# One step's shift of the compressed exponential's followers in the samples' attention of a hybrid decoder kernel

## The reference

```
s_c = einsum(q, k_cmp) * scale                       # compressed scores, 63 blocks
p_c = masked_softmax(s_c)                            # the compressed exponential
o_c = einsum(p_c, v_cmp)
imp = einsum(p_c, overlap)                           # importance of each block of 64 rows
score = where(forced, 1e9, where(future, -1e9, imp))
_, idx = top_k(score, 8)                             # which blocks are attended
s_s = einsum(q, gathered k_sel)                      # here: all scores, with a mask from the top 8
p_s = masked_softmax(s_s)                            # the selected exponential
o_s = einsum(p_s, gathered v_sel)
p_w, o_w = the same over the last 256 rows           # window branch
o = gate_c * o_c + gate_s * o_s + gate_w * o_w
```

## Time and profile before

| what | value |
|---|---|
| median of 3 runs | 4016.66 us (4012.67 to 4022.57) |
| profiled execution, its own time | 4024.7 us |
| its span | 4022.5 us |
| PE busy / PEld busy | 3844.9 us (96%) / 3509.6 us (87%) |
| DVE busy / ACT busy / POOL busy | 50% / 28% / 42% |
| mean granted TensorE clock | 0.978 of full |

### The profile page before, as it was taken

One profiled execution on the slowest core, in us unless ns is written; L12 is line 12 of the kernel. 1 busy time (PEld: TensorE's weight loads), 2 busy tenths in 40 slices (PEclk: granted clock), 3 DMA queues, 4 the chain that ended last, 5 costly groups with the idle time before them and its releaser, 6 DMA issues. The chain is left out here.

```text
span 4022.5 us, 83836 instructions
## 1 busy us (share of the span) xinstructions
PE 3844.9 (96%) x34280; PEld 3509.6 (87%) x34280; DVE 2019.4 (50%) x4755; ACT 1114.4 (28%) x2470; POOL 1695.1 (42%) x2284
## 2 busy tenths in 40 slices
PE   8998899989999999999999988999899999999997
PEld 8987788866699999999899787888666999999997
DVE  6587544457535414414456865444574454143153
ACT  3154233347721000000212532333477210000011
POOL 5633222136754434434355322222377644344342
PEclk9999899999999999999999999999899999999998
DMA  3254433220031131131322543332200411311312
GB/s 130 84 166 163 117 92 90 69 96 7 13 123 65 45 124 53 48 132 44 113 91 88 159 170 106 84 87 71 95 9 21 133 50 46 132 48 60 120 37 94
DMA packets 201777, 349.65 MB, mean 87 GB/s; under 512 B 72899, under 2 KB 135491, under 8 KB 200515
## 3 DMA queue, kind: packets, MB, share of 16 engines
q1 hardware_dynamic: 201394, 344.29, 27.1%
HBM read 253.03 MB, written 95.90 MB: 87 GB/s over the span
## 5 line engine op out<-in xcount | busy, mean ns | idle before, releaser
L2599 POOL CAST wr_hi<-wr_raw 128x256 fp32r<-128x256 f32 x584 | 264.9, 454 | 903.9 <-PE ps L2634 898.4
L2601 POOL TENSOR_TENSOR wr_lo<-wr_raw,wr_hi 128x256 fp32r<-128x256 f32 x584 | 548.5, 939 | 46.8
L2634 PE MATMUL ps<-xh,wr_hi 128*128 128x384 f32 x2064 | 453.6, 328 | 0.0
L2634 PE MATMUL ps<-xl,wr_hi 128*128 128x384 f32 x2064 | 453.1, 327 | 0.0
L2634 PE MATMUL ps<-xh,wr_lo 128*128 128x384 f32 x2064 | 453.0, 327 | 0.0
L1374 POOL TENSOR_TENSOR rc_CT<-rc_AT,rc_masks 128x256 f32<-128x256 f32 x192 | 136.4, 730 | 528.5 <-DVE rc_AT L1409 411.9
L2687 ACT ACTIVATE de_c<-de_c 128x1088 f32<-128x1088 f32 (+1 forms) x44 | 49.0, 1114 | 1098.1 <-DVE de_c L2783 1098.1
L2634 PEld LDWEIGHTS ps<-xh,wr_hi 128*128 128x128 f32 x2064 | 349.0, 188 | 0.3
L2634 PEld LDWEIGHTS ps<-xl,wr_hi 128*128 128x128 f32 x2064 | 348.9, 188 | 0.0
L2634 PEld LDWEIGHTS ps<-xh,wr_lo 128*128 128x128 f32 x2064 | 348.8, 188 | 0.0
L2634 PE MATMUL ps<-de_mixh,wr_hi 128*128 128x384 f32 (+3 forms) x1440 | 321.4, 331 | 8.1 <-DVE de_mixl L2722 8.1
(11 more groups left out here) (452 smaller groups left out, 7611.3 us busy)
## 6 DMA issues: line engine op xcount, KB each, us to landing
sa_kvp<-in_cache SPq DMA_DIRECT2D x128, 256.0 KB
scr_xres<-de_x SPq DMA_DIRECT2D x56, 544.0 KB, 2.7
de_x<-scr_xres SPq DMA_DIRECT2D x56, 544.0 KB, 3.6
wr_raw<-in_w_gate SPq DMA_DIRECT2D x42, 512.0 KB, 3.6
wr_raw<-in_w_up SPq DMA_DIRECT2D x42, 512.0 KB, 3.6
rc_arbk<-scr_arbk SPq DMA_DIRECT2D x32, 512.0 KB, 4.5
wr_raw<-in_w_down SPq DMA_DIRECT2D x32, 512.0 KB, 3.6
pr_raw<-in_w_rw SPq DMA_DIRECT2D x28, 512.0 KB, 4.4
```

The lines of the kernel that those rows point to most:

```text
L2599: pool.tensor_copy(hi[:, k, :], raw[:, k, :]).then_inc(w_hi, 1)
L2601: pool.tensor_tensor(lo[:, k, :], raw[:, k, :], f32(hi[:, k, :]), ALU.subtract).then_inc(w_ready, 1)
L2634: m = pe.matmul(ps[:, (bank + b) * BANK:(bank + b) * BANK + cols], w[rows, k, :], x[rows, k, o:o + cols], start=(k == 0 and i == 0), stop= ...
```

## The change

On all engines the steps around the block scores are shifted. PE: L1563 to L1568 go from step 10 to step 11, and L1573 to L1580 from step 11 to step 12; L1587 stays in step 14. ACT: the copies L1648 to L1650 go from step 10 to step 11; the selected exponential L1655 stays in step 13. DVE: L1732 to L1738 go from step 9 to step 10, L1741 to L1744 from 10 to 11, L1746 and L1747 from 11 to 12, and the mask L1752 to L1757 from step 12 to step 13, that is, into the same step as the exponential that waits for it; L1762 on stay in step 14. Nothing is added or removed.

```diff
@@ sample_tensor
                 m.then_inc(s_scored, 1)
                 yield
+                yield
                 pe.wait_ge(imp_ready, c + 1)
...
                 m.then_inc(w_out, 1)
                 yield
                 yield
-                yield
                 pe.wait_ge(s_exp, c + 1)
```

## The result

The changed kernel takes 4057.3 us (4055.96 to 4064.44 in 4 runs) and the kernel before 4016.42 (4012.67 to 4022.57 in 4 runs): ratio 1.0096, 95% interval 1.0084 to 1.0108. In a second comparison it was 4052.54 against 4020.22, ratio 1.0073 (1.0058 to 1.0089). It is slower by 0.7 to 1.0%, 32 to 41 us; forecast were 28 us, 4045, in a range of 4024 to 4060.

What follows compares the result with a forecast made beforehand. PE, busy for 96% of the span, was taken to bound the kernel, so only its idle time could move. Median 4016.7 + 16 us of later transposes + 12 us of clock falls = 4045 us, 4024 to 4060 eight times in 10.

Steps and rivals of the forecast that it cites:

- the forecast's own 4036 to 4056: Whole kernel: the range given to the main forecast of 4045 us, which had a chance of 0.50.
- the rival in which the clock falls in all blocks or stays low for longer: Samples' blocks: PE's clock falls in all or stays low longer, 16 + 20 us and more, 4053 to 4070; chance 0.10.
- Both terms of the sum: The two stages: 16 us of later transposes and 12 us of clock falls, added to the median.
- The chain of 2.91 us from mask to L1587: Block 5: mask 1.57 us, then 1.34 to PE's L1587; the order cannot shorten it, only delay the mask's start.
- The wait at L1587: Sign, 471 to 832 us: PE's wait for the exponential L1655 should grow from 3.6 to 13 to 17 us.
- The wait of L1279 for L1426: Sign, 471 to 832 us: PE's wait for the scan's DVE work should stay at 3 to 5 us.
- the working of block 4: Block 4: idle 0.69 us ahead of L1313 goes, mask stands behind L1446, L1587 at 678.14 instead of 676.54: 1.6 us lost.
- The first sum: Later L1587 over the eight blocks: 8.05 us in a layer, 16 in both, bounds 10 to 22.
- The clock term: Behind L1587 in blocks 0, 1, 4, 5, 7: 4 more falls a layer at 1.5 us, 12 us in both.
- The rival that rested on it: Samples' blocks: the clock does not fall more often, only the first sum is left, 4033 us (4028 to 4036); chance 0.25.
- The rival on the other side: DVE, step 13: mask reached early, L1279's wait of 4.0 us a layer goes, L1587 waits as before, 4009 us; chance 0.04.

Runs made afterwards that it cites:

- the dense filling: Changed kernel plus matmuls without use on PE ahead of the selected transposes, in pairs on the array's two halves, 16 to 46 a block: 4041.84 us, ratio 1.0066.

## Why the prediction was right

- **PE bounds the stage, and its idle time moves: right.** The order changed, not the work, and all the loss of the two traces lies in the two stages: half in PE's waits, half in the clock behind them, which the forecast had as a term of its own.
- **The time lies at the upper end of what was said.** 4057.3 us is inside the range to 4060, but over the forecast's own 4036 to 4056 and inside the 4053 to 4070 of the rival in which the clock falls in all blocks or stays low for longer. That rival had a chance of 0.10 and came half true: the clock falls in seven blocks of eight, in block 0 for twice as long. Both terms of the sum were too small, as the next points say; only in the second comparison is the loss, 32 us, near the 28 of the forecast.
- **The chain of 2.91 us from mask to L1587, with the mask behind the scan's DVE work: right, and shown** by the two experiments that moved the mask alone, back and forth. Block 5 lost 2.3 us (2.3 forecast), block 0 1.4 (1.35), block 6 0.5 (0.5), block 7 1.8 (1.4), block 1 gained 0.3 (a loss of 0.1 forecast), block 2 lost 0.5 (0.2). The wait at L1587, forecast at 13 to 17 us, is 14.9. The wait of L1279 for L1426, which was to stay at 3 to 5 us, fell to 2.6.
- **Blocks 3 and 4 mis-sized: 1.3 and 2.4 us instead of 0.6 and 1.6.** The step that failed is the working of block 4, which took the idle time ahead of L1313 as gained. It did not ask when the block scores are ready, now that DVE computes them in step 10. There they stand behind the scan's additions, and PE's next group, L1299, is short. The rows after, block 4, PE and DVE, and DVE's row before:

```profile
674.07 0.63 PE L1299 MATMUL ps<-rc_S,rc_arbk 64*64 64x64 f32 x16
675.58 0.29 PE L1564 MATMUL ps<-sa_im,sa_cm 64*64 64x17 f32 x2 [0.87 <-DVE sa_im L1739]
```

```profile
673.82 0.89 DVE L1428 TENSOR_TENSOR rc_XX<-rc_XX,ps 128x256 f32<-128x256 f32 x2 [1.64 <-PE ps L1291]
...
675.34 0.18 DVE L1739 TENSOR_TENSOR sa_im<-sa_im,sa_pg 64x17 f32<-64x17 f32 x1
```

```profile
669.80 0.18 DVE L1738 TENSOR_TENSOR sa_im<-sa_im,sa_pg 64x17 f32<-64x17 f32 x1
```

  DVE idles 1.64 us ahead of L1428, in which the four operations stood before (the last at 669.80, L1428 at 670.05). Putting them back gave 0.9 us in each of the two blocks. The first sum was 8.05 us in a layer and measured 9.9.
- **The clock term: the mechanism right, the count too low.** 4 more falls in a layer were forecast, at 1.5 us; there are 6 more, and block 0's lasts twice as long. Blocks 2, 3 and 6, which I had left out for waits under 2 us, have one each; block 1, which I had counted for a wait of 2.1 us or more, waits 1.29 us (1.21 before) and has none. The working had given it 0.1 us of loss, so its wait could not have grown to 2.1. One fall costs 1.2 to 1.6 us. The term was 12 us and measured 18.7. Two slips in the working change nothing: half of 0.84 behind 717.56 is 717.98 and not 717.93, and all other blocks are 14 falls, 21 us, not 13 and 20.
- **The rule of the clock page.** By the Trainium skill ("TensorE: Matmul & The Clock Gate", section "HAM oscillation — how this bites in real kernels") the waits would have been too short for a fall. The trace does not agree: there are 14 falls in the samples' blocks, with waits at L1587 of 0.98 to 2.82 us. The rival that rested on it, 4033 us without a clock term, is refuted.
- **The rival on the other side** is refuted too: the gain that it named is real (4.0 to 2.6 us at L1279), but the transposes do wait.

What stays open is what decides in the doubtful blocks. In both traces of the changed kernel block 1, with a wait of 1.29 us, keeps its clock and block 6, with the same wait, does not, though PE is as busy in the 4 us up to L1587 (blocks 1 and 6 of layer 0):

```profile
533.00:537.00 4.00, 2.67 (x70) 2.26 (x67) 3.79 (x16) 1.99 (x4) 1.45 (x2) 1.00 0.03 9
780.50:784.50 4.00, 2.67 (x69) 2.24 (x66) 3.79 (x16) 1.99 (x4) 0.00 (x0) 1.00 0.02 4
```

Nor is it a property of the block: with the mask alone put back, the clock falls in block 1 of layer 0 (0.50 from 536.8 to 540.1 us) and not in block 1 of layer 1 (1.00), behind the same work:

```profile
532.80:536.80 4.00, 2.71 (x70) 2.33 (x67) 3.35 (x15) 2.08 (x5) 1.23 (x2) 0.99 0.02 4
...
2523.40:2527.40 4.00, 2.71 (x70) 2.33 (x67) 3.35 (x15) 2.08 (x5) 1.23 (x2) 1.00 0.02 4
```

The same holds for blocks 0 and 1 of the kernel before. So the wait and the work around it do not decide alone. Something that differs between the layers has a part, for instance the moment at which the wait comes; which it is stays open, since no experiment varied the moment by itself. That a filled wait takes 12 of 14 falls away is shown; which of the shorter waits brings one cannot be forecast from these runs.

## What to carry to other kernels

Where engines are interleaved by hand, a step that is moved on one engine lands behind the other job's work of that step: count the time from the last thing that the moved work now stands behind to the instruction that waits for it, block by block, since a pattern of 16 steps against one of 19 meets another neighbour each time. For the same reason no single order was best, and choosing it for each block gave 0.4% that no uniform shift gave. When short waits open on TensorE amid thin work, price the clock as well: here it doubled the loss.

## What the runs showed of the hardware that was not expected

- The clock does not follow the busy share of the profile. With PE busy for 4.00 of 4 us by single matmuls of 64 columns with weight loads of 64x128 (37 records) it fell (0.51 in the next window). In the dense filling, block 4, with 115 records in 4 us, PE busy for 3.95, it was 1.00 and stayed so:

```profile
680.00:684.00 4.00, 3.95 (x115) 3.63 (x111) 1.92 (x12) 1.87 (x4) 0.00 (x0) 1.00 0.14 33
684.00:688.00 4.00, 3.89 (x92) 3.53 (x92) 2.37 (x7) 0.37 (x2) 0.00 (x0) 1.00 0.03 8
```

- A transpose of 64 columns costs PE 0.07 us in these blocks, a matmul of the same f32 shape two passes of 0.11 us.
- Up to L1587 the samples' blocks of the changed kernel repeat between its two traces to 0.02 us, and between the layers too, but for block 3 (12.07 us in layer 0, 12.21 or 12.22 in layer 1). The rest of the program does not: its sum goes from 3257 to 3270 us in the profiles of kernels that are the same there, which is as much as the runs of one kernel spread.
